# Moving the start of the V-block loads from the SyncE queue to ScalarE in the expert stages of a hybrid diffusion backbone

## What is computed

```python
def expert_block(args):
    hb, eb, gb = args
    a = jnp.einsum('tkd,td->tk', u_tab[eb], hb)
    w = (jax.nn.gelu(a.astype(jnp.float32)) * gb).astype(hb.dtype)
    return jnp.einsum('tk,tkd->td', w, v_tab[eb])
```

## Time and profile before

| | us |
|---|---|
| median of three runs | 5581.73 (5578.24 to 5589.88) |
| the profiled execution | 5594.32 |
| its span | 5592.5 |
| VectorE busy, whole span | 4288.9 (77%) |
| TensorE busy, whole span | 4695.5 (84%) |
| ScalarE busy, whole span | 1806.6 (32%) |

### The profile page before, as it was taken

How to read it: one execution, slowest core, us unless ns; L and a number is a source line. 1 busy time by engine, 2 the same in 40 slices (tenths; PEclk the granted TensorE clock), 3 DMA queues, 4 the chain that set the end, 5 groups by cost and what they waited for, 6 DMA issues and landing times. The chain is left out here.

```text
span 5592.5 us, 68247 instructions
## 1 busy us (share of the span) xinstructions
PE 4695.5 (84%) x22838; PEld 3737.5 (67%) x22838; DVE 4288.9 (77%) x7460; ACT 1806.6 (32%) x3290; POOL 987.5 (18%) x714
## 2 busy tenths in 40 slices
PE   7886839888886659999999879889696659999997
PEld 3765728534764548888898738744575548888886
DVE  5456488667546879999999868758634989999997
ACT  2232311131232653333333321221122654444443
POOL 0000017300000003333333216400000002222221
PEclk9887969899997879999999989999898769999999
DMA  5432329602122569999999829611121249999996
GB/s 214 177 111 78 135 73 367 224 23 83 49 71 98 166 191 378 390 387 384 389 396 386 329 98 341 247 47 64 53 87 60 61 145 372 375 375 378 382 376 240
DMA packets 458291, 1230.36 MB, mean 220 GB/s; under 512 B 210227, under 2 KB 244308, under 8 KB 396950
## 3 DMA queue, kind: packets, MB, share of 16 engines
q1 hardware_dynamic: 355896, 613.96, 31.8%
q0 software_dynamic: 102240, 614.51, 27.9%
HBM read 1168.78 MB, written 59.51 MB: 220 GB/s over the span
## 5 line engine op out<-in xcount | busy, mean ns | idle before, releaser
L2597 POOL DMA_INDIRECT arena<-in_peer_uv,kept x448 | 636.6, 1421 | 3393.6 <-POOLq L2448 1981.4
L233 PE MATMUL psum<-v_ring_hi,w_parts 128*128 128x512 f32 x2560 | 838.1, 392 | 9.7 <-DVE v_lo L2703 9.7
L233 PE MATMUL psum<-h_hi,u_ring_hi 128*128 128x384 f32 (+1 forms) x2048 | 671.7, 328 | 41.8 <-DVE u_lo L2698 41.1
L233 PE MATMUL psum<-h_hi,u_lo 128*128 128x384 f32 (+1 forms) x2048 | 664.3, 324 | 0.0
L233 PE MATMUL psum<-h_lo,u_ring_hi 128*128 128x384 f32 (+1 forms) x2048 | 663.4, 324 | 0.0
L2738 DVE SCALAR_TENSOR_TENSOR arena<-arena 128x1024 f32<-128x1024 f32 x448 | 558.6, 1282 | 19.2
L2728 DVE CUSTOM_DVE_ANT_0 arena<-arena 128x1024 f32<-128x1024 f32 x448 | 536.3, 1221 | 42.7 <-DMA arena<-in_peer_uv,kept 42.2
L233 PEld LDWEIGHTS psum<-v_ring_hi,w_parts 128*128 128x128 f32 x2560 | 482.8, 189 | 106.8 <-DVE v_lo L2703 11.4
L233 PE MATMUL psum<-v_lo,w_parts 128*128 128x512 f32 x1280 | 502.7, 393 | 0.0
L233 PEld LDWEIGHTS psum<-h_hi,u_ring_hi 128*128 128x128 f32 x2048 | 385.6, 188 | 89.3 <-DVE u_lo L2698 43.3
L233 PEld LDWEIGHTS psum<-h_lo,u_ring_hi 128*128 128x128 f32 x2048 | 386.0, 188 | 5.4 <-issue 0.5
(11 more groups left out here) (390 smaller groups left out, 9503.0 us busy)
## 6 DMA issues: line engine op xcount, KB each, us to landing
kept<-in_mix SPq DMA_DIRECT2D x312, 512.0 KB, 3.5
kept<-in_peer_u SPq DMA_DIRECT2D x256, 512.0 KB, 6.8
kept<-in_peer_uv SPq DMA_DIRECT2D x256, 512.0 KB, 5.7
kept<-in_ada SPq DMA_DIRECT2D x96, 512.0 KB, 4.4
gate_scratch<-arena SPq DMA_DIRECT2D x11, 4096.0 KB, 20.9
arena<-gate_scratch SPq DMA_DIRECT2D x64, 384.0 KB, 5.7
arena<-gate_scratch SPq DMA_DIRECT2D x64, 320.0 KB, 8.5
spec_scratch<-arena POOLq DMA_DIRECT2D x4, 2048.0 KB, 11.0
```

The lines of the kernel that those rows point to most:

```text
L233: done = pe.matmul(out, lhs[x], rhs[y], start=first and j == 0, stop=last and j == 2)
L2597: pool.indirect_dma_start(rows[q % NBUF], None, peer_uv, bass.IndirectOffsetOnAxis(ap=at, axis=0))\
```

## The change

The V load leaves SyncE's step and is issued in ScalarE's step, behind `gelu(k+2)` and ahead of `round_v(k+1)`. It waits for the same semaphore value as before. The loads of U and of the gates stay where they were, so that in SyncE's list they now follow each other directly. Nothing that is computed changes.

```diff
@@ -2562,10 +2562,6 @@
                     def step(b, k, at):
                         if at_most(b, k, NK - 3):
                             load_u(b, k + 3)
-                        if at_most(b, k, NK - 2):
-                            sp.wait_ge(v_split.sem, v_split.at(b + (k + 1)))
-                            sp.dma_start(ring[:, 2 + k % 2, :], peer_uv[ds((b + (l * NK + k + 2)) * P, P), D:2 * D])\
-                              .then_inc(loaded[2 + k % 2].sem, 16)
                         if k % 2 == 1 and at_most(b, k, NK - 4):
                             sp.wait_ge(w_ready.sem, w_ready.at(b + (k + 1)))
                             load_gates(b, k + 3)
@@ -2679,6 +2675,9 @@
                            .then_inc(gelu_ready.sem, 1)
                         if at_most(b, k, NK - 2):
                             gelu(b, k + 2)
+                            act.wait_ge(v_split.sem, v_split.at(b + (k + 1)))
+                            act.dma_start(ring[:, 2 + k % 2, :], peer_uv[ds((b + (l * NK + k + 2)) * P, P), D:2 * D])\
+                               .then_inc(loaded[2 + k % 2].sem, 16)
                         if at_most(b, k, NK - 1):
                             round_v(b, k + 1)
 
```

## The result

The changed kernel takes 5710.89 us (median of four runs, 5703.19 to 5718.66) against 5584.39 us for the kernel before on the same chip: a ratio of 1.023, 95% interval 1.0206 to 1.0254. It is 126 us slower. I had forecast 5599 us, and a range of 5545 to 5640.

What follows compares the result with a forecast made beforehand. VectorE's own work was taken as the floor, with waits for transfers as an excess on it. Layer 0's 4, layer 1's 7 and late V's 6 gave +17 us, thus 5599 us, range 5545 to 5640.

Steps and rivals of the forecast that it cites:

- The issue on ScalarE: Ahead of `round_v`: issuing V leaves 0.22 us a step uncovered in layer 0, 0.29 in layer 1; 65 us in full.
- the absorption: Both layers: steps already waiting for transfers take up the issue's delay, leaving 4 us in layer 0, 10 in layer 1.
- no effect: Layer 0: U and V moved in time neither shorten nor lengthen the gathers; bounds -19 and +28 us.
- My even spread: Excess of a pair of steps spread evenly from zero to twice its mean: 0 to 1.48 us layer 0, 0 to 1.04 layer 1.
- my signs of being wrong: `gelu` to `round_v` below 0.5 us, ScalarE's DMA row far longer than SyncE's, or gather waits of layer 0 rising.
- V's lead: V issued later, 7.05 us ahead of use in layer 1, about 8.0 in layer 0; late loads cost +6 us in layer 1.
- Rival 3: Layer 1: V's own queue stretches its landing beyond 7.05 us, 0.5 us in each of 128 steps; 5657 us, chance 0.13.
- U and the gates sooner: U starts about 2 us sooner, removing ScalarE's 28.7 us wait in layer 1; the layer's +10 us becomes +7.
- Rival 2: Both stages: transfers bound them, so added issue time fills existing waits and nothing changes; 5582 us, chance 0.22.
- Rival 1: Both layers: waits vanish as the burst ahead of the gathers breaks up, issue nearly covered; faster, 5540 us, chance 0.27.

Runs made afterwards that it cites:

- the small store: Kernel before with U and gates early and V early on SyncE, plus a 64-byte store issued on ScalarE where the change starts V: 5559.9 us, ratio 0.9959.
- the late start: Against the kernel before: V on SyncE's queue but held until `gelu` of its block, U and gates early: 5658.1 us, ratio 1.0137.
- the queue: The change with V still on ScalarE's queue but issued early, at the end of `rest_v`; U and gates early: 5610.1 us, ratio 1.0051 to the kernel before.
- the queue alone: Against the kernel before: V on ScalarE's queue at the head of its step, U and gates held until `rest_v`: 5625.7 us, ratio 1.0068.
- the early run on SyncE: Against the kernel before: V stays on SyncE at its old time, U and gates go out early, no longer behind V: 5555.8 us, ratio 0.9946.

## Why the prediction was wrong, point by point

**The issue on ScalarE: right in size, wrong in what became of it.** 0.22 us uncovered in layer 0 was met to the hundredth in the step shown; over the stretch it is 0.22 to 0.31. In the single steps of layer 1, where I had 0.29, nothing is uncovered: the DMA starts at 4899.73, ahead of the small GELU (4899.83) and of `gelu` (4899.92), and `round_v` keeps its 0.32 us. There the sequencer had run ahead of two instructions that stood behind the running `round_u`. In layer 0, and in the double steps of layer 1, the DMA row comes 0.17 us behind the start of `gelu`; in these steps the small GELU had waited for VectorE, 0.7 us or more. So I was right for layer 0, and wrong to carry its row over to layer 1. The rule of the Trainium skill that I set aside (Perfetto Trace Analysis, DVE / Act Engine Instruction) has the sequencer go on past an instruction that waits for its semaphores, too. No step here shows that: it ran ahead only where the small GELU had nothing to wait for.

**Layer 0: two steps failed, the absorption and "no effect".** I let 28 us of added floor cost 4, since steps that wait for a gather would have something to give. They gave about half. Against the run with the issue behind `round_v`, the change has 34.5 us of waits for `round_v` and 17.1 us less of waits for gathers (41.4 and 58.5), and it is 13 us slower in layer 0; the small store shows the same ratio. That there is something to give fits the kernel: `rows_free` of step k starts the gather for step k+2, so a longer step k+1 gives it more time. My even spread from zero to twice the mean gave too much.

The larger error is that I took the moved loads to have no effect on layer 0, with +28 us as the upper bound of the layer. It cost 44 us. With nothing in front of `round_v` the waits for gathers rose from 35.6 to 58.5 us. In the change itself they rose to 41.4, which was one of my signs of being wrong. Of the 44, some 8 are the late start (8.65 against 8.59), 15 the queue (8.71 against 8.59) and 13 the issue; some 8 come only when they stand together, and the cause of these is open.

**V's lead: the term that was mis-sized most.** This is the main failure. I took 6 us from the landing times of before: a sixth of the loads late, by 0.6 us. Measured are waits in nearly every double step, 79.7 us in 784.8, and layer 1 as a whole lost 87 us. My 7.05 us of lead were about right (7.56 in the step above). What failed is that I kept the old landing, 6.1 us, for a load that starts at another moment and in another queue. The V loads for double steps landed after 5.7 us before, 6.2 when early on SyncE, 8.2 when late there and 9.3 in the change (medians). Rival 3, with 0.13, had the mechanism in part: V's own queue does stretch its landing (from 6.1 to 6.9 us in "the queue alone"), but the larger part comes with the later start. Its price of 64 us was too low, as half a microsecond in each step was an arbitrary bound: the waits are 1.7 us (79.7 / 46) in every other step.

**U and the gates sooner: right mechanism, small number.** The wait for U in layer 1 went, 25.9 to 2.4 us in the stretch. Alone, with V early on SyncE, it is worth 30 us (5556), where I had taken 3. In the change the wait for V takes its place.

**Rival 2, the bound by transfers,** fell three times: without gates the step of layer 0 is no shorter, the early run on SyncE shortened layer 1 with every byte still moved, and the change lowered the DMA share of layer 1 to 0.91 (0.99 before). Its rule from the Trainium skill (DMA: Bandwidth & Descriptors, Issuing engines are not separate DMA queues) says that another issuing engine only saves time of issue. The runs agree that it brings no bandwidth: "the queue alone" moved 376 and 372 GB/s in the two stretches, against 389 and 376 before. They also show that it isn't free: this run is 0.68% slower.

**Rival 1** was right that the waits for U vanish and that this can make the kernel faster, but the change wasn't the edit that did it. That breaking up the burst ahead of the gathers helps is not shown: the early run on SyncE leaves layer 0 at 8.59 us, against 8.60.

## What to carry to other kernels

Before you move the start of a load, compare its new lead with the landing time at its new moment, not with the median of the old place; starting V near `gelu` raised it here from 6.2 to 8.2 us on the same queue, in the steps that count. Look at each kind of step by itself: here only the double steps waited. Don't count on waits for transfers to swallow a delay; here they took about half of it. When two loads stand in one queue with different conditions, put the one that becomes ready first in front; that cost nothing here and beat both kernels.

## What was unexpected in the hardware

A load moved to a queue of its own, at its old time, made the whole kernel 0.68% slower (with U and the gates half a microsecond sooner), or 54 us slower where nothing but the queue differs. The landing of the same 512 KB on the same queue depends on its moment and on what stands ahead of it. In layer 1 of the early run on SyncE two V loads that follow each other, the first sent 2.7 us behind the gates, the second with no gates ahead of it, land like this:

```profile
DMA to landing us min/median/max: 11.1/11.1/11.1
...
DMA to landing us min/median/max: 6.5/6.5/6.5
```

It did no harm there, as both had 11.9 us. And a busy DMA share of 0.99 did not mean that the transfers bound the kernel: with 6% of the bytes taken away (393 KB of gates in 6.68 MB of a pair of steps), layer 0 kept its step, and with all of them moved layer 1 went from 7.41 to 7.18 us.
